# A two-block transformer-like model in one kernel: high and low products of wide weight blocks, ordered in pairs

## What is computed

```python
h = h + y @ w_out[l]                                   # 2048 x 2048
a = rmsnorm(h) @ w_up[l]                               # 2048 -> 2 x 5632, then a short convolution
h = h + (silu(gate) * val) @ w_down[l]                 # 5632 -> 2048
...
h = h + concatenate([y_ssd, y_rwkv]) @ w_out_2[l]      # 4096 -> 2048
v = rms_norm(h, norm2_g[l])
h = h + (silu(v @ w_gate[l]) * (v @ w_up[l])) @ w_down_2[l]
```

## Time and profile before

| | |
|---|---|
| median of 3 runs | 2926.92 us (2925.81 to 2929.77) |
| the profiled execution | 2923.5 us |
| its span, first to last instruction | 2921.7 us |
| mean granted TensorE clock | 0.995 |
| PE, PEld busy | 97%, 86% |
| DVE, ACT, POOL busy | 69%, 53%, 25% |
| HBM traffic | 162 GB/s over the span |

### The profile page before, as it was taken

How to read it: one execution, slowest core, us unless ns; L and a number is a source line. 1 busy time by engine, 2 the same in 40 slices (tenths; PEclk the granted TensorE clock), 3 DMA queues, 4 the chain that set the end, 5 groups by cost and what they waited for, 6 DMA issues and landing times.

```text
span 2921.7 us, 52438 instructions
## 1 busy us (share of the span) xinstructions
PE 2834.7 (97%) x21110; PEld 2521.4 (86%) x21110; DVE 2020.4 (69%) x3265; ACT 1554.2 (53%) x2581; POOL 735.7 (25%) x878
## 2 busy tenths in 40 slices
PE   8989999999999999999999999999999999999998
PEld 8868988888888888888888888988888888888887
DVE  7674887765777666777777777777676665566654
ACT  7345555544555555466666655465454444444443
POOL 1343212110112230776566520023121110011112
PEclk9999999999999999999999999999999999999999
DMA  6314555556555566422222323445555555655554
GB/s 251 105 59 158 174 189 191 193 169 198 200 189 190 172 200 210 145 77 98 99 102 95 106 95 109 161 179 173 189 184 192 193 186 179 205 188 189 188 179 151
DMA packets 80047, 475.40 MB, mean 163 GB/s; under 512 B 8256, under 2 KB 11328, under 8 KB 38720
## 3 DMA queue, kind: packets, MB, share of 16 engines
q1 hardware_dynamic: 76768, 459.72, 46.1%
q10 hardware_dynamic: 3040, 12.32, 1.2%
HBM read 465.72 MB, written 6.29 MB: 162 GB/s over the span
## 4 chain that ended last, share of the span: by engine, by line
PE 75%; DVE 13%; ACT 5%; POOL 4%; issue 3%; DMA 0%; ACTq 0%; SPq 0%; POOLq 0%; DVEq 0%
PE bank L784 36%; PE bank L788 22%; PE bank L786 3%; DVE m L1343 3%; PE bank L787 3%; PE bank L777 3%; ACT m L2230 2%; POOL m L2979 2%; POOL m L2975 1%; DVE m L2015 1%; DVE m L1389 1%; PE bank L897 0%; ACT m L2629 0%; PE bank L1135 0%; DVE m L1931 0%
## 5 line engine op out<-in xcount | busy, mean ns | idle before, releaser
L788 PE MATMUL bank<-m,m 128*128 128x256 f32 x6624 | 1854.8, 280 | 0.0
L784 PE MATMUL bank<-m,m 128*128 128x512 f32 x4736 | 1644.5, 391 | 6.6 <-DVE m L1343 5.5
L1343 DVE TENSOR_TENSOR m<-m,m 128x1024 fp32r<-128x1024 f32 (+1 forms) x912 | 1037.0, 1145 | 577.8 <-ACT m L2230 570.9
L788 PEld LDWEIGHTS bank<-m,m 128*128 128x128 f32 x6624 | 1248.2, 188 | 0.1
L2230 ACT ACTIVATE m<-m 128x1024 fp32r<-128x1024 f32 (+1 forms) x912 | 878.5, 977 | 637.2 <-PE bank L788 610.9
L784 PEld LDWEIGHTS bank<-m,m 128*128 128x128 f32 x4736 | 889.0, 188 | 201.4 <-issue 4.0
L786 PE MATMUL bank<-m,m 128*128 128x256 f32 x1888 | 555.0, 294 | 19.2 <-DVE m L1343 16.5
L787 PE MATMUL bank<-m,m 128*128 128x256 f32 x1888 | 527.8, 280 | 0.0
L786 PEld LDWEIGHTS bank<-m,m 128*128 128x128 f32 x1888 | 359.0, 190 | 39.0 <-issue 29.3
L787 PEld LDWEIGHTS bank<-m,m 128*128 128x128 f32 x1888 | 357.7, 189 | 1.2
L2948 POOL TENSOR_TENSOR m<-m,m 128x256 fp32r<-128x256 f32 x44 | 63.5, 1443 | 548.0 <-ACT m L2530 548.0
(11 more groups left out here) (380 smaller groups left out, 2813.1 us busy)
## 6 DMA issues: line engine op xcount, KB each, us to landing
m<-in_w_up SPq DMA_DIRECT2D x88, 1024.0 KB, 4.8
m<-in_w_down SPq DMA_DIRECT2D x128, 704.0 KB, 4.1
m<-in_w_gu SPq DMA_DIRECT2D x88, 1024.0 KB, 4.8
m<-in_w_out SPq DMA_DIRECT2D x48, 1024.0 KB, 5.2
m<-in_w_krv SPq DMA_DIRECT2D x48, 1024.0 KB, 4.8
m<-in_w_xbc SPq DMA_DIRECT2D x24, 1024.0 KB, 4.8
m<-in_w_z SPq DMA_DIRECT2D x16, 1024.0 KB, 4.8
m<-in_w_in SPq DMA_DIRECT2D x14, 1024.0 KB, 6.0
```

Of the source, the lines that this page charges most:

```text
L784: pe.matmul(bank.rearrange("p (a b) -> p a b", a=2), hi, x, start=kc == L.k0, stop=False)
L788: m = pe.matmul(ps, lo, x[:, 0, :], start=False, stop=last)
L1343: v.tensor_tensor(lo_of(k), raw_of(k)[0], hi_of(k).bitcast(F32), SUB).then_inc(*lo_v(("lo", k)))
```

## The change

The low products of a wide layer are taken two blocks at a time. Within a piece, `c = w // 128` is the block's number. Each block issues its high product of 512 columns. At odd `c`, and at the last block of a piece, the low products follow: of the block before and of this one (at a last block with even `c` only its own). The low products' operands, the bank, the accumulation and the semaphores' place (the last product of the piece or the tile) stay. Narrow layers are as before; only their low product is moved into the branch.

```diff
                         hi, lo = hi_of(j)[:, w:w + 128], lo_of(j)[:, w:w + 128]
                         if L.wide:
+                            c = w // 128
                             pe.matmul(bank.rearrange("p (a b) -> p a b", a=2), hi, x, start=kc == L.k0, stop=False)
+                            if c % 2 == 1 or L.ends(t, kc):
+                                for n in range(c // 2 * 2 - c, 1):
+                                    m = pe.matmul(ps, lo_of(j)[:, w + 128 * n:w + 128 * n + 128], rhs(kc + n)[:, 0, :],
+                                                  start=False, stop=last and n == 0)
                         else:
                             pe.matmul(ps, hi, x[:, 0, :], start=kc == L.k0, stop=False)
                             pe.matmul(ps, hi, x[:, 1, :], start=False, stop=False)
-                        m = pe.matmul(ps, lo, x[:, 0, :], start=False, stop=last)
+                            m = pe.matmul(ps, lo, x[:, 0, :], start=False, stop=last)
```

## The result

The changed kernel takes 2950.68 us (median of 4 runs, 2949.52 to 2952.69) against 2927.62 before: ratio 1.0080, 95% interval 1.0067 to 1.0093. It is slower by 23 us. The profiled execution took 2952.69 us.

A forecast was written before the change was run, and what follows sets the result against it. TensorE's closed stream of wide products, bounded by its own spacing, was taken as the bound. All terms came to 0 us against the profiled 2923.5; with the median 3.4 above, the forecast was 2927, range 2896 to 2942.

The forecast's parts named there:

- What bounds the kernel: TensorE's wide stretches: a closed stream of matmuls bounded by their own spacing, 4736 blocks, 1642 us, 56% of the span.
- 256 after 256 does not uncover a load: Between a pair's low products: both loads stay covered, worth 0; if not, 71 ns a pair, +164 us, chance 0.01.
- the sum over the pair: Four gaps of each of 2304 wide pairs: two keep their price, two new ones taken at about 0; total 0 us.
- keep their neighbours' kinds: Wide pair's gaps 512 then 256 and 256 then 512: same kinds as before, so no change counted.
- a slot appears to belong to its own instruction and not to its neighbour: Ground for taking 512 after 512 in the wide pair at 0, between -34 and +15 us.
- the narrow stream's rows as prices: 256 after 256 priced from narrow blocks, 0.1178 or 0.1133 us each: +0.9 to -9.4 us, taken as about 0.
- The mean of the two narrow paces: Narrow blocks of three 256s at 0.3533 and 0.3400 us; their mean, 0.3467, costs the same as a wide block.
- time goes by columns: Three narrow 256s at their mean pace cost the same as a wide block of 768 columns, 0.3467 us.
- Rival (c): The slow pace takes hold in the wide pair: slower, 2957 in full or 2942 halfway; chance 0.17.
- its full price: Slow pace in both new gaps of the wide pair: 13.3 ns a pair, +31 us, 2957.
- two loads in a row with no slack: Argument for the slow pace: two 256s in a row, where now every second load has 0.1 us of slack.
- Rival (b): 512 after 512 in the wide pair is cheaper, a gap below 0.225: up to -34 us, 2893; chance 0.11.

The follow-up runs named there:

- eights: The change carried to whole pieces, eight high products and then eight low ones, against the kernel before: 2948.79 us, ratio 1.0076.
- blocks turned round: Kernel before with every second block reversed (high c, low c, low c+1, high c+1): 2942.82 us, ratio 1.0055, when repeated after a disturbed first measurement.
- all 512: Kernel before with the low half multiplied with both rows of the activations, so 512 + 512 columns with two loads: 3488.54 us.
- two lows: Kernel before with a second low product of 256 columns and its own load, so 512 + 256 + 256: 3485.27 us.
- the low halves' exchange: Kernel before with the low products of a pair's two blocks exchanged (high c, low c+1, high c+1, low c): 2927.85 us, ratio 1.0004.
- `w_up` moved: Activations of `w_up` alone 32 bytes further on: 2943.59 us (ratio 1.0051) in the changed kernel, 2935.23 (1.0036) in the kernel before.

## Why the prediction was wrong

I forecast 2927 with 2896 to 2942, and it is 2950.7, outside the range.

- What bounds the kernel: right, but for one reading: L788 of the earlier trace rows holds the narrow layers' low products too, so its 58% are not the wide stream's alone; the 1642 us, 56%, are. The loss is all in the spacing of the wide products; no wait, load, ACT, DVE or DMA has a part in it (idle before L785 7.5 us). That 256 after 256 does not uncover a load was right too: gaps of 0.118 to 0.120 between the low products, and with a third load for the same columns no more time.
- **The step that failed** is the sum over the pair: two of the four gaps "keep their neighbours' kinds" and so their price, and of the two others the 512 after a 512 is taken at 0. The ground was that "a slot appears to belong to its own instruction and not to its neighbour". Measured, the pair lost 10.0 ns in the first halves and 13.3 in the second ones. The gap from 512 to 256, held to be untouched, has the greater part, 5.4 and 8.4 ns; 512 after 512 has 3.7 and 2.5, 256 after 256 has 0.9 and 2.5. So a gap depends on more than its two products. The strict turn is a pattern with a pace of its own at that place, 0.3467. Every order that left it altogether (pairs, eights, blocks turned round, all 512, two lows) had 0.350 to 0.3533 in `w_up` for 768 columns; the low halves' exchange, which keeps the turn, kept the pace.
- Behind it lies a second fault: I took the narrow stream's rows as prices for the wide one. Their operands lie 32 bytes nearer to the weights' place, and there the ranking of the orders is another. The mean of the two narrow paces, 0.3467, equalled the wide pace by accident, as far as the runs show, and I built on it that time goes by columns and that a slot belongs to its own instruction. The first holds within 4% (0.3400 to 0.3600 for 768 columns), the second doesn't.
- Rival (c) was the right case, with chance 0.17. Its mark, 0.70 us or more for a pair, is there in `w_up` and `w_gu`; its full price of 13.3 ns a pair was paid in their second halves (0.7065), 10 in the first halves and in `w_out2`, and 8 in the two `w_down` layers (5.1 us over 640 pairs). In sum that is 24 us, between its half price of 15 and its full price of 31. The range took in only the half. But its ground, two loads in a row with no slack, is not what happened: with `w_up` moved the same two loads follow each other and the pair costs nothing.
- Rival (b), a cheaper 512 after 512, did not come true here, where it took 0.232 to 0.233. In `w_up` moved it comes near its mark of 0.225, with 0.226, but the 256 behind takes back as much (0.236), and the pair has the turn's 0.6933.

What the runs don't settle: by what mechanism the distance and the order work. The Trainium skill (SBUF — State Buffer, Who interferes with whom) gives TensorE two independent read ports, for the moving operand and for the weights, and has it wait for no one. No run here shows the ports; but moving the weights alone by 32 bytes cost 28 us, so the two reads are not free of each other in this kernel, or something else ties their places together. Only the old distance and those 32 bytes less and more were tried, and not every order at each; whether 64 bytes would bring the old pace back is open. Nor is it settled why the halves of `w_up`, with the same code and places, have 0.3517 and 0.3533 in the changed kernel.

## What to carry to other kernels

Where a stream of fp32r products is closed, with no waits, expect its pace to be a property of order and place together; here that was 1 to 2% of the wide stream and 1% of the kernel either way. After changing the order, move the moving operand (or the weights) by 32 bytes and measure both places; after moving a tile, measure the orders again. Prices for an operation should come from rows with the same operands' places, not only the same shape.

## What was unexpected of the hardware

- Some paces come back exactly in stretch after stretch: 0.3400, 0.3467 and 0.3533 us for 768 columns, 0.4667 for 1024 (two lows). These four are whole multiples of 6.67 ns (51, 52, 53 and 70); others, as 0.3517, 0.352 and 0.356, are not.
- With the weights moved and the activations of the narrow layers not, their blocks took 0.3546 us on average, never 0.3400. With the distance of the kernel before most of their unbroken stretches run at 0.3400 or at 0.3533 throughout, and after a pause it can be the other. The stretch of `w_out`, PE alone, in the kernel before and in the changed one, whose code is the same there:

```profile
282.00:320.00 38.00, 38.00 (x325) 1.00 0.64 206
```
```profile
282.00:320.00 38.00, 38.00 (x337) 1.00 0.65 217
```

325 against 337 products in 38 us; from start to start 0.3533 and 0.3400 us for three. The 220 blocks of the two long stretches of `w_out` have the slow pace in the one profile and the fast one in the other, 220 x 13.3 ns = 3 us. By this estimate such changes can make some us of difference between executions of one kernel; no run varied them alone.
